# Layer 1's gate rows and one modulation turn are issued inside the attention's last steps

## The reference

```python
mod_l = (c_act @ mod_w[i] + mod_b[i]).reshape(b, N_MOD, 1, d)
...
# layer 1: 4 heads of latent attention, then 4 heads of differential attention
o_m = attend(q_m, k_m, v_m, MLA_SCALE)
a1 = attend(q1, k1, v_d, DIFF_SCALE)
a2 = attend(q2, k2, v_d, DIFF_SCALE)
o_d = rms_norm(a1 - lam.astype(a1.dtype) * a2, g_sub) * (1.0 - lam_init)
yl = jnp.concatenate([o_m.reshape(b, l, -1), o_d.reshape(b, l, -1)], axis=-1) @ w_out
...
xl = xl + mod_l[:, 2] * yl                               # the attention gate
h2l = modulate(rms_norm(xl, norm_g[i, 1]), mod_l[:, 3], mod_l[:, 4])
...
xl = xl + mod_l[:, 5] * moe(h2l, ...)                    # 32 experts, top 2 of one group
```

## Time and profile before

| | |
|---|---|
| median of 3 runs | 970.32 us (969.63 to 970.88) |
| the profiled execution | 970.78 us |
| its span, first to last instruction | 969.1 us |
| PE busy | 859.2 us, 89% |
| DVE, ACT, POOL busy | 324.4, 170.1, 171.3 us |
| mean granted TensorE clock | 0.961 |
| read from HBM | 293.66 MB |

### The profile page before, as it was taken

The page is one execution under the profiler, slowest core; times in us unless marked ns, Lnnn a source line. Parts: engine busy times, 40 slices in busy tenths (PEclk is TensorE's granted clock), DMA queues, the critical chain, the costliest instruction groups (busy, mean ns, idle before and its releaser), DMA issues.

```text
span 969.1 us, 10234 instructions
## 1 busy us (share of the span) xinstructions
PE 859.2 (89%) x3863; PEld 380.2 (39%) x3863; DVE 324.4 (33%) x711; ACT 170.1 (18%) x419; POOL 171.3 (18%) x210
## 2 busy tenths in 40 slices
PE   1899999999999999788679999898799999778786
PEld 0444445448333333222266444454546333222222
DVE  1279997226110211111132432647205121011001
ACT  2301023125000000000041113445314000000000
POOL 2100391221220222220222212201010111011001
PEclk9999999999999999998879999999799999999889
DMA  9999354709999999999897042544727999999993
GB/s 364 406 382 398 143 220 185 306 18 324 329 406 400 371 403 376 415 413 419 330 411 298 1 173 88 231 204 174 325 110 260 350 406 410 415 420 426 412 419 161
DMA packets 33686, 297.99 MB, mean 308 GB/s; under 512 B 6528, under 2 KB 6834, under 8 KB 16220
## 3 DMA queue, kind: packets, MB, share of 16 engines
q1 hardware_dynamic: 26640, 283.26, 72.5%
q0 software_dynamic: 6912, 13.92, 4.1%
q10 hardware_dynamic: 76, 0.02, 0.0%
HBM read 293.66 MB, written 12.58 MB: 316 GB/s over the span
## 4 chain that ended last, share of the span: by engine, by line
PE 51%; DMA 19%; DVE 14%; issue 6%; ACT 3%; SPq 2%; PEld 2%; POOL 1%; another core or an unknown queue 0%; PEldq 0%; POOLq 0%; DVEq 0%
PE bank L1223 14%; DVE WORK L2122 9%; DMA ring<-in_gu_pack 9%; PE bank L468 9%; PE bank L1246 6%; PE bank L1369 5%; DMA B<-in_gu_pack 5%; PE bank L1101 3%; PE bank L997 2%; SPq L946 2%; DMA ring<-in_mod_pack 2%; PE bank L1316 2%; DMA WORK<-x_old,smalli 1%; DMA h_rows<-B 1%; PE bank L1035 1%
## 5 line engine op out<-in xcount | busy, mean ns | idle before, releaser
L1223 PE MATMUL bank<-ring,hT 128*64 128x512 f32 x688 | 209.6, 630 | 25.6 <-DMA ring<-in_gu_pack 17.8
L2036 DVE SCALAR_TENSOR_TENSOR hT<-hT,WORK,bank 128x256 f32<-128x256 f32 x34 | 16.3, 480 | 329.4 <-ACT hT L1522 323.0
L1223 PEld LDWEIGHTS bank<-ring,hT 128*64 128x64 f32 x688 | 61.8, 144 | 120.2 <-issue 120.0
L2122 DVE SCALAR_TENSOR_TENSOR WORK<-WORK,par 128x512 f32<-128x512 f32 x116 | 90.7, 859 | 0.0
L468 PE MATMUL bank<-ring,hT 128*128 128x512 f32 (+2 forms) x256 | 88.0, 499 | 0.7 <-ACT hT L1485 0.7
L1246 PE MATMUL bank<-ring,WORK 128*64 128x512 f32 x368 | 83.5, 595 | 1.6 <-ACT WORK L1527 1.6
L1223 PE MATMUL bank<-WORK,hT 128*64 128x512 f32 x128 | 59.9, 610 | 5.9 <-issue 4.3
L997 PE MATMUL bank<-ring,cs 128*32 128x512 f32 x384 | 48.8, 641 | 16.3 <-DMA ring<-in_mod_pack 15.3
L1527 ACT ACTIVATE WORK<-bank 128x256 f32<-128x256 f32 x34 | 13.1, 384 | 283.0 <-PE bank L1232 283.0
L1223 PE MATMUL bank<-X,hT 128*64 128x512 f32 x112 | 56.2, 650 | 6.1 <-DMA B<-in_gu_pack 4.7
L468 PEld LDWEIGHTS bank<-ring,hT 128*128 128x128 f32 x256 | 46.0, 190 | 35.9 <-issue 34.0
(11 more groups left out here) (295 smaller groups left out, 1054.1 us busy)
## 6 DMA issues: line engine op xcount, KB each, us to landing
ring<-in_gu_pack SPq DMA_DIRECT2D x38, 2048.0 KB, 23.1
ring<-in_mod_pack SPq DMA_DIRECT2D x24, 2048.0 KB, 16.4
ring<-in_down_pack SPq DMA_DIRECT2D x22, 2048.0 KB, 25.2
WORK<-in_gu_pack SPq DMA_DIRECT2D x6, 2048.0 KB, 31.2
ring<-in_wout_pack SPq DMA_DIRECT2D x4, 2048.0 KB, 14.6
ring<-in_gu_pack SPq DMA_DIRECT2D x8, 1024.0 KB, 27.9
ring<-in_win_pack SPq DMA_DIRECT2D x3, 2048.0 KB, 37.6
X<-in_gu_pack SPq DMA_DIRECT2D x3, 2048.0 KB
```

The source lines that it names most:

```text
L1223: mm = pe.matmul(dst[ST * x:ST * x + ST, :], HG[L][s][:, k, :], columns(units[x], 512 * k, 512), start=k == 0, stop=k == KC - 1)
L2036: dve.scalar_tensor_tensor(out=T1[L][s], in0=SG[L][s], scalar=cwt[:, at:at + 1], in1=src[:, 0:DE], op0=ALU.mult, op1=ALU.mult).then_inc(se ...
L2122: ins = dve.scalar_tensor_tensor(out=acc, in0=src, scalar=w, in1=acc, op0=ALU.mult, op1=ALU.add)
```

## The change

The eight gate products move from behind the attention into step 16, behind the turn of the last probabilities, and go to banks 0 and 1 in place of 4 and 5, once the exponentials of unit 14 are done. The turn of row 10 moves into step 17. On ACT the copy of row 11 moves into step 16 and the two copies of the gate rows into step 17. The turn of row 11 stays behind step 18.

```diff
@@ attention_pe
                 if 0 <= i - 1 < n_units:
                     probs(i - 1)
+                if i == n_units:
+                    pe.wait_ge(sem("exp_done"), n_units - 1)
+                    gates("a1", 1, 2, (1,), (0, 1))
+                elif i == n_units + 1:
+                    mod_turn(10)
@@ attention_scalar
                 if 0 <= i - 1 < n_units:
                     turned_probs(i - 1)
-            mod_copy(11)
+                if i == n_units:
+                    mod_copy(11)
+                elif i == n_units + 1:
+                    gate_rows("a1", (1,), (0, 1))
@@ tensor
-            attention_pe(pe, mod_turn, mod_in_attention)
-            mod_turn(10)
-            gates("a1", 1, 2, (1,), (4, 5))
+            attention_pe(pe, mod_turn, mod_in_attention, gates)
             mod_turn(11)
@@ scalar
-            attention_scalar(act, mod_copy)
-            gate_rows("a1", (1,), (4, 5))
+            attention_scalar(act, mod_copy, gate_rows)
```

More of the change, by code:

```diff
@@ L512, in project_pe, with attention_pe @@
                     turn(i - 2)
-        def attention_pe(pe, mod_turn, mod_in_attention):
+        def attention_pe(pe, mod_turn, mod_in_attention, gates):
             pe.wait_ge(sem("cols"), count(99, NORMED))
@@ L574, in attention_pe, with attention_scalar @@
                     probs(i - 1)
-        def attention_scalar(act, mod_copy):
+                if i == n_units:
[3 more added lines that the diff above has]
+                    mod_turn(10)
+        def attention_scalar(act, mod_copy, gate_rows):
             def cols(i):
```

## The result

The changed kernel takes 963.99 us (median of 5 runs, 962.69 to 966.4) beside 970.32 (968.36 to 970.88) before. The ratio is 0.994, with a 95% interval of 0.9927 to 0.9954: 5.8 us faster, 4.5 to 7.1 by the interval (the two medians themselves lie 6.3 us apart). The forecast was 4.8 us.

What follows compares the result with a forecast made beforehand. PE bounds the changed stretch, the weight stream the expert stage. 6.22 us leave, less 0.45, plus 0.2: projection starts 5.97 earlier; less 1.2 for the clock, gain 4.8, so 965.5 us, range 961.6 to 968.8.

Steps and rivals of the forecast that it cites:

- The sum: At the projection: it starts 5.97 us earlier and ends 4.8 us earlier, 1.2 going back to the low clock.
- The small terms: Around the last output turn: gate products take 1.83 us, delay some 0.45; turn 10 and the gate rows on ACT free.
- this course of things alone: The forecast itself, without the rivals: 965.5 us, band 964.2 to 967, chance 0.62.
- The clock: In the projection: falls near 691.7 as before, stays low 5.7 us into the dense work, losing 2.85 us.
- Rival B: Attention's end to projection: the clock doesn't fall, the holes being partly filled; gain 8.3, 962.0 us; chance 0.18.
- The 5.7 us borrowed from the last weight wait: In the projection: low clock lasts 5.7 us into the dense matmuls, as in the burst from 931.7 to 937.4.
- Rival C: In the attention's last steps: clock already low before the gate products; gain 2.0 to 3.2, 967.3 to 968.5 us; chance 0.12.
- Whether it reaches the end: Behind the projection: routing, gathers and the weight stream's start hang on one chain, so all 4.8 us pass through.
- Rival D: Behind the projection: the rows' store falls behind a 2 MB weight piece if SP leads by over 0.69 us; 975.3; chance 0.08.
- what leaves the path: Behind the attention: the wait and turn 10 take 2.67 us, the gate products 3.55, together 6.22; turn 11 stays.

Runs made afterwards that it cites:

- the exchanged order: Kernel before with two statements behind the attention swapped: gate products first, then turns 10 and 11, nothing moved into the attention; 968.07 us, 0.9987.
- the early product: Changed kernel with the projection's first product issued behind turn 10, before the last output turn, and the gate products back behind the attention; 962.68 us, 0.9932.

## Why the prediction was right, and where it was not

**The sum.** The projection was to start 5.97 us earlier, and did by 6.32 and 6.34 (first pair of profiles 16.37 to 10.05, second pair 16.03 to 9.69). It was to end 4.8 us earlier, and did by 5.13 and 4.84. Luck has a part in so close a fit: which two executions make a pair is chance, and crossed the gain at the end is 3.16 or 6.81 us. The small terms were right too: the gate products 1.79 us where 1.83 stood, the last output turn at 690.98 less 0.28 of late arrival, so 0.2 us of delay where 0.45 stood (the products started 0.14 us sooner behind the turned probabilities than I let them), turn 10 and the gate rows on ACT (689.72 to 690.80) without cost. The measured 5.8 us is more than the forecast of 4.8, which lies inside its interval, and 963.99 us is 0.2 below the band of 964.2 to 967 that was given to this course of things alone.

**The clock.** Rival B did not come: the clock fell in both looks at the changed kernel. The 5.7 us borrowed from the last weight wait were met in one execution (5.7) and not in the other (3.0). As a size it belongs to an execution, not to the kernel, and the kernel before has the same spread: 3.3 us of the projection in one look, none in the other. Rival C (low already before the gate products) was not seen in a changed kernel. The first look at the exchanged order shows only that the clock can fall in the last hole, at 687.0 and before the last output turn. The times of C were also added up 0.2 us too high: 970.32 less 2.0 to 3.2 is 967.1 to 968.3.

**Whether it reaches the end.** It does, within what single profiles can tell. 5.13 us at the projection's end became 4.58 at the span's end in the first pair, 4.84 became 5.45 in the second. The half with only turn 10 gained 6.97 at the projection's end against the first profile of before, and 7.23 at the span's end. Between the projection's end and the span's end pass 240.65 to 241.98 us in eleven profiles, and 243.32 to 243.62 in the three with the low clock on the last instructions. Rival D did not come: SP issued the piece for `X` at 735.59, now 0.19 us ahead of the store and not 0.02 behind, but D needed more than 0.69, and the store landed in 11.06 us.

**The step that failed** is "what leaves the path", in how it shares out the 6.22 us. It priced the gate products at 3.55 us and turn 10 with its wait at 2.67, as if each were worth its own length. From that the expectations for the halves came to 2.7 us for the gate products and 2.3 for turn 10; they measured 0.9 and 5.4. At the projection's start the halves gain 2.73 and 5.34 us, together 8.07, and the whole change 6.32. Most of what is counted twice is the 1.76 us that the low clock added to the gate products before: each half saves it, the whole can save it only once. Smaller terms (turn 11 at full clock in one half, the new wait of 0.36 us in the other) roughly cancel. Half of the 3.55 was not work but low clock, and it went without the products being moved, once the wait and turn 10 no longer followed the last output turn. Moving the products in addition takes 1.0 to 1.3 us from the projection's start (11.03 to 10.05 and 9.69), but leaves only a four-column turn between the last output turn and the projection; in both looks the clock fell again and took that back (end 38.58 and 38.57 with the products behind, 40.42 and 38.74 with them inside). The sum came out right because the whole change contains the half that works, and because the low clock in the projection was in the sum.

What stays open: why the exchange of two statements loses the clock even where it was up through the gate products, while the half with only turn 10 moved keeps it in three looks of three (twice by itself, and once with the early product). Turn 10 fills the hole and leaves the stretch behind the attention in one step, so the runs do not tell which of the two does it; row 11's copy moved early with turn 10 left behind was not run. They show the difference, not its rule.

## What to carry to other kernels

When a stretch runs at the low clock, the length of a job in it is not what moving the job is worth. Look for what stands around the fall, move one job at a time, and look again at what the rest costs. A hole is best filled with full-width products that were to come anyway, here the first product of the next stage: it saved its own 0.86 us, and the clock was up in all three profiles with such a product (with an unused one it was up in the changed order and fell in the old one). And take a second profile before a clock that fell at one place is called a property of the kernel.

## What the runs showed that I had not expected

The granted clock falls at different moments in executions of one program: 691.4 and 692.0 in the changed kernel; 687.0 and 693.8 in one look at the exchanged order, 695.9 in the other. The end of the projection differs by 1.4 to 2.0 us between two such executions (43.10 and 41.65; 40.42 and 38.74; 45.55 and 43.58), where the five times of the changed kernel span 3.7 us. The busy share of the profile did not foretell a fall: the clock held with PE busy for 3.90 of 7.65 us in the half with only turn 10 moved, and fell after 5.71 of 8.10 in the change.

```profile
681.20:688.85 7.65, 3.90 (x31) 3.61 (x32) 2.26 (x7) 3.68 (x13) 1.48 (x4) 1.00 0.97 371
```
